# An encoder block on eight cores: LN1 and the squares leave GpSimd, the roots come to it, with a deeper ring and another last tile

## The reference, cut to what matters

```python
proj = einsum('bsd,de->bse', x, w_in)          # 1792 columns: q, k, v, gu, gv
attn = banded_window_attention(q, k, v, sink)  # |t-s| <= 128, 8 query heads on 2 kv heads
gu, gv = gelu(gu), gelu(gv)
sgu = gu * (w_s @ layer_norm(gv) + b)          # in chunks of 128 positions, 8 channel groups
mixed = concat(rms_norm(attn), rms_norm(sgu))  # 512 + 512
x = layer_norm(ALPHA * x + mixed @ w_out)      # LN1
h = square(relu(x @ w_ff1))                    # 4096 wide
x = layer_norm(ALPHA * x + h @ w_ff2)          # LN2
```

## Time and profile before

| what | us |
|---|---|
| median of three runs | 2795.45 (2789.4 to 2796.35) |
| the profiled execution, its own time | 2794.41 |
| its span, core 2, the slowest | 2792.8 |
| the other cores' spans | 2781.2 to 2792.4 |
| TensorE busy in the span | 2645.5 (95%) |
| VectorE, ScalarE, GpSimd busy | 1491.9, 1072.5, 955.4 |

### The profile page before, as it was taken

One profiled execution on the slowest core, in us unless ns is written; L12 is line 12 of the kernel. 1 busy time (PEld: TensorE's weight loads), 2 busy tenths in 40 slices (PEclk: granted clock), 3 DMA queues, 4 the chain that ended last, 5 costly groups with the idle time before them and its releaser, 6 DMA issues.

```text
span 2792.8 us, 57164 instructions; the slowest of 8 cores (2781.2 to 2792.8 us)
## 1 busy us (share of the span) xinstructions
PE 2645.5 (95%) x20844; PEld 1706.4 (61%) x20844; DVE 1491.9 (53%) x2558; ACT 1072.5 (38%) x2241; POOL 955.4 (34%) x661
## 2 busy tenths in 40 slices
PE   4689999999999999999999998899999999999996
PEld 2357777777677777777777676775444444444442
DVE  5876776767777777677767574111222221233222
ACT  4445555555555555555555452221111110111111
...
GB/s 264 220 128 111 103 80 100 110 88 96 99 102 86 107 95 92 100 103 88 107 97 102 80 92 133 156 189 121 151 164 138 147 141 153 177 159 136 157 106 76
DMA packets 110134, 345.81 MB, mean 124 GB/s; under 512 B 11680, under 2 KB 11680, under 8 KB 99744
## 3 DMA queue, kind: packets, MB, share of 16 engines
...
## 4 chain that ended last, share of the span: by engine, by line
PE 78%; ACT 6%; DVE 6%; issue 4%; DMA 4%; POOL 2%; DVEq 0%; ACTq 0%; SPq 0%; POOLq 0%
PE psum L836 27%; PE psum L804 23%; PE psum L760 8%; PE psum L659 4%; PE psum L673 4%; PE psum L675 4%; DMA hsc<-arena 2%; PE psum L729 2%; ACT L678 1%; PE psum L716 1%; DVE arena L689 1%; DMA arena<-w_gu 1%; PE psum L665 1%; PE psum L667 1%; PE psum L754 1%
## 5 line engine op out<-in xcount | busy, mean ns | idle before, releaser
L804 PE MATMUL psum<-arena 128*128 128x256 bf16 x8192 | 999.6, 274 | 15.8 <-ACT arena L648 9.8
L836 PE MATMUL psum<-arena 128*128 128x512 bf16 x4096 | 891.5, 379 | 4.5 <-POOL arena L858 2.3
L804 PEld LDWEIGHTS psum<-arena 128*128 128x128 bf16 x8192 | 773.2, 98 | 163.0 <-issue 56.1
L836 PEld LDWEIGHTS psum<-arena 128*128 128x128 bf16 x4096 | 399.5, 98 | 491.0 <-issue 16.6
L809 POOL TENSOR_TENSOR arena<-arena 128x512 bf16<-128x512 f32 x256 | 268.9, 1050 | 699.8 <-ACT arena L807 402.1
L807 ACT ACTIVATE arena<-psum 128x512 f32<-128x512 f32 x512 | 302.8, 592 | 370.7 <-PE psum L804 341.1
L774 POOL TENSOR_TENSOR arena<-arena 128x1024 f32<-128x1024 f32 x128 | 309.2, 2415 | 301.4 <-DVE arena L771 273.3
L843 DVE SCALAR_TENSOR_TENSOR arena<-psum,arena 128x512 f32<-128x512 f32 x128 | 88.3, 692 | 593.2 <-PE psum L836 521.6
L646 ACT ACTIVATE arena<-arena 128x1 f32<-128x1 f32 x320 | 93.3, 293 | 782.4 <-DVE arena L849 660.1
L856 POOL TENSOR_TENSOR arena<-arena 128x1024 f32<-128x1024 f32 x62 | 145.7, 2351 | 558.9 <-ACT arena L853 558.9
L809 DVE TENSOR_TENSOR arena<-arena 128x512 bf16<-128x512 f32 x256 | 214.7, 838 | 173.4 <-ACT arena L807 90.5
...
## 6 DMA issues: line engine op xcount, KB each, us to landing
hsc<-arena SPq DMA_DIRECT2D x256, 256.0 KB, 2.5
...
arena<-xt POOLq DMA_DIRECT2D x64, 256.0 KB, 5.2
...
```

The costliest lines, as they stand in the source:

```text
L804: R.pe(lambda e, fc=fc, ph=ph, z=z: [e.matmul(ph.ap[:, z * 256:(z + 1) * 256], lhsT=w1q[fc // 4].ap[:, c, (fc % 4) * 128:(fc % 4 + 1) * 12 ...
L836: R.pe(lambda e, s_=s_, q=q: [e.matmul(ps[s_][hf].ap, lhsT=hb[fc // 16].ap[:, fc % 16, s_ * 128:(s_ + 1) * 128], rhs=w2c[fc // 4].ap[:, fc ...
```

## The change

The roots: `rsqrt` now issues two GpSimd operations on one element per partition, an add of the epsilon and a power of -0.5. The `rms_norm` roots take the sum of squares as it is; the factor sqrt(512) goes into the VectorE operation that applies the root. LN1's end is two VectorE operations on 1024 elements, `(y - mean) * G1` and `y * rstd + B1`. The square of bank `k` = 1 is ScalarE's, and each half of a stage has a record of its own. The last three tiles of `ff1` write to a ring of 8 stages that lies over `hT[1]`. In the last tile, `ff2_last` finishes one bank after the other, normalises with the same two VectorE operations per half row, and writes four pieces of 256 KB, from SP and ScalarE in turn.

```diff
+    NHXT = 3
...
+    for g in range(2):
+        ap = A2.alloc(BF16, [16, 256])
+        t = Buf(ap, f"hT1_{g}", extra=A.under(*A2.last))
+        hxgate_w = t.extra
+        flat = ap.rearrange("p a b -> p (a b)")
+        for k in range(4):
+            hx.append(Buf(flat[:, k * 1024:(k + 1) * 1024], f"hx{g}{k}"))
...
-    def rsqrt(src_ap, src_buf, eps_buf, scale, lnb, outb):
-        R.act(lambda e: e.activation(out=lnb.ap, in_=src_ap, func=AF.Ln, bias=eps_buf.ap, scale=scale),
-              [src_buf, eps_buf], [lnb], 60, "el")
-        R.act(lambda e: e.activation(out=outb.ap, in_=lnb.ap, func=AF.Exp, scale=-0.5), [lnb], [outb], 1, "el")
+    def rsqrt(src_ap, src_buf, eps, outb):
+        R.pool(lambda e: e.tensor_scalar(out=outb.ap, in0=src_ap, scalar1=eps, scalar2=None, op0=ALU.add), [src_buf], [outb], 50)
+        R.pool(lambda e: e.tensor_tensor(out=outb.ap, in0=outb.ap, in1=mhalf.ap, op=ALU.pow), [outb, mhalf], [outb], 50)
...
-        R.dve(lambda e: e.tensor_scalar(out=yb.ap, in0=yb.ap, scalar1=mv1[p].ap[:, 0:1], scalar2=rstd1[p].ap,
-                                        op0=ALU.subtract, op1=ALU.mult), [yb, mv1[p], rstd1[p]], [yb], 1024, 2)
-        for (cst, aop) in ((G1, ALU.mult), (B1, ALU.add)):
-            R.pool(lambda e, cst=cst, aop=aop: e.tensor_tensor(out=yb.ap, in0=yb.ap, in1=cst.ap, op=aop), [yb, cst], [yb], 1024)
+        R.dve(lambda e: e.scalar_tensor_tensor(out=yb.ap, in0=yb.ap, scalar=mv1[p].ap[:, 0:1], in1=G1.ap,
+                                               op0=ALU.subtract, op1=ALU.mult), [yb, mv1[p], G1], [yb], 1024)
+        R.dve(lambda e: e.scalar_tensor_tensor(out=yb.ap, in0=yb.ap, scalar=rstd1[p].ap, in1=B1.ap,
+                                               op0=ALU.mult, op1=ALU.add), [yb, rstd1[p], B1], [yb], 1024)
...
+            if i >= NI - NHXT:
+                j = hn[0] % len(hx)
+                hs, h2, hkey, hg = hx[j], hx2[j], f"hx{j}", [hxg]
...
-                eng = R.dve if k == 0 else R.pool
-                eng(lambda e, hs=hs, r_=r_, k=k: e.tensor_tensor(out=hs.ap[:, k * 512:(k + 1) * 512], in0=r_.ap, in1=r_.ap,
-                                                                 op=ALU.mult), [r_], [hs], 512)
+                if k == 0:
+                    R.dve(lambda e, hk=h2[k], r_=r_: e.tensor_tensor(out=hk.ap, in0=r_.ap, in1=r_.ap, op=ALU.mult),
+                          [r_] + hg, [h2[k]], 512)
+                else:
+                    R.act(lambda e, hk=h2[k], r_=r_: e.activation(out=hk.ap, in_=r_.ap, func=AF.Square), [r_] + hg, [h2[k]], 480)
...
+    def ff2_last(i):
...
+        for s_ in range(2):
...
+            for hf in range(2):
...
+                for q in range(8):
+                    R.pe(lambda e, s_=s_, q=q, hf=hf: [e.matmul(ps[s_][hf].ap, lhsT=hb[fc // 16].ap[:, fc % 16, s_ * 128:(s_ + 1) * 128],
...
+                R.dve(lambda e, hf=hf, y_=yh[hf]: e.scalar_tensor_tensor(
+                    out=y_.ap, in0=ps[s_][hf].ap, scalar=1.0 / ALPHA, in1=y_.ap, op0=ALU.mult, op1=ALU.add),
...
+            rsqrt(mvB[p].ap[:, 1:2], mvB[p], EPS / (ALPHA * ALPHA), rstdB[p])
+            for hf in range(2):
+                R.dve(lambda e, hf=hf, p=p, y_=yh[hf]: e.scalar_tensor_tensor(
+                    out=y_.ap, in0=y_.ap, scalar=mvB[p].ap[:, 0:1], in1=G2.ap[:, hf * 512:(hf + 1) * 512],
...
+                R.dma("sp" if hf == 0 else "act", lambda e, s_=s_, hf=hf, y_=yh[hf]: e.dma_start(
```

64 lines of the change are left out of this document (51 added, 13 removed).

## The result

The changed kernel takes 2836.7 us (the median of three runs, 2834.6 to 2837.1; a fourth of 3199.6 us, with cores 4 to 7 at a granted clock of 0.82 to 0.83 in place of 0.98, is left out, as such runs are of every ratio below) where the kernel before takes 2795.7: a ratio of 1.015, 95% interval 1.013 to 1.017. That is 42 us slower, where 30 us faster was predicted, and 47 us above the upper end of the range. In what follows a ratio is turned into us by (ratio - 1) x 2795.

A forecast was written before the change was run, and what follows sets the result against it. TensorE was taken as the bound, busy 1462.4 of 1500 us in the long stretch, with gains only where it waits. Terms -15 - 3 + 0 + 2 + 1 - 14 = -29 took 2794.4 us to 2765, range 2746 to 2790.

The forecast's parts named there:

- The step that failed first: Long stretch, 200 to 1700 us: TensorE does the same matmuls after the change, so at most its idle 37.6 us can be won.
- the root's price: Roots on GpSimd: two operations taken at 0.3 us each, the latency as unchanged from ScalarE's 0.293 + 0.200 us.
- The second rival: Roots come late on GpSimd, queued behind waiting transfers, and hold VectorE: 0.8 us a block, 2816 us; chance 0.13.
- Long stretch, -15: 200 to 1700 us: TensorE's three waits of 24.7 us lose two causes, 15 us off; bounds 25 off or nothing.
- Start, -3: Up to 200 us: casts lose at most 9.2 us of stretching, LN1s add 6.5; -3, between -9 and +5.
- Transition, 0: 1700 to 1780 us: no gain, since the ring serves only later tiles 29 to 31; bounds -8 to +10.
- the bound of +10: Transition's upper bound: ScalarE, now also waiting for the transfers that empty `hst`, holds relus back.
- Handover, +2: Handover to second half: loading `hT[1]` must wait for the last stores of h; +2 us, 0 to 8.
- the last sign of being wrong: The prediction is wrong if TensorE stands still around 1900 us for `hT`.
- Second half, +1: Roots can queue behind GpSimd's wide operations, but TensorE has another tile to work on; +1 us, 0 to 4.
- Tail, -14: Kernel's end: 4.1 us off for gap and slow start, 10.1 in place of 20.1 after; 14 off, 9 to 15.
- the views named as a test: New profile: L689's successor near 0.54 us, casts 0.68 to 0.8, no late gap, 10 us end, `hst` waits remaining.

The follow-up runs named there:

- e1: The changed kernel with the constant -0.5 put in the word of the unused epsA, so later buffers lie 4 bytes lower, as before the change: ratio 1.0064.
- e9: On e1, the planner told GpSimd's measured root times (254 and 740 ns in place of twice 305), only the order changing: ratio 1.0005.
- e7: On e1 with its old planner costs, all roots back on ScalarE as logarithm and exponential: ratio 0.9928.
- e15: On e7, the ring of store slots switched off (NHXT 0), nothing else: ratio 0.9908, 2767.1 us.

## Why the prediction was wrong

**The step that failed first** stands in the first paragraph, on what bounds the kernel: TensorE "does the same matmuls after the change". It does the same ones, but those of seven lines at 2.2 to 2.5 ns more in the mean. The diff had the cause in plain sight, one word allocated ahead of every buffer, and I gave it no cost since no row of before shows an operand's place. It cost 24 to 28 us, in the long stretch 91.0 - 75.4 = 15.6 and in the second half 25.2 - 20.2 = 5.0.

**The second step that failed is the root's price.** I took 0.3 us an operation, between a memset of 0.10 and a wide operation of 2.4; the two took 0.254 and 0.741 in the mean. The prediction itself gave one sign of it: wrong if VectorE shows long waits for roots. The latency was not "unchanged": in the last tile but one of after 1.2 us pass from the end of the statistics to the operation that takes the root. With the planner's price it made the 34 to 38 us of the roots.

The second rival, to which I gave 0.13, said 2816 us, and the change without its word (e1) is at 2813 by its ratio. That nearness is partly luck, since its mechanism, roots held up behind transfers in GpSimd's stream, shows in one root of four. In the long stretch of after (core 4, by the starts in the trace) the roots behind L705, L716 and L787 begin 0.16 to 0.17 us (median) after what they wait for; the attention's, behind L759, begins 0.74 us after it, in 23 blocks with the issue of x's load (L570) in between. Beyond 0.3 us each, these delays make 24 us; in e9 they make 23, so they are not what the planner's price won there.

The terms, by the stages of the table, first with the roots back and the word out (e7), then as changed:

- *Long stretch, -15.* -9.6 in e7, +21.6 as changed. The mechanism was right: the waits for L689's successor and for the relu went, VectorE's operations run at 0.547 us. Two thirds of the size came in e7. With the roots on GpSimd not even that did: the scores' waits, 18.2 us in after, are 18.7 in e1 and 1.7 in e7.
- *Start, -3.* -4.9 in e7, 0.1 in e1, +3.5 as changed. The casts lost 22 x (1.100 - 0.727) = 8.2 us, against 9.2 at most.
- *Transition, 0.* -4.4 in e7, +1.6 as changed, inside its bounds. ScalarE did come to wait for the slots (14.9 us) and to hold relus back, as the bound of +10 had it: TensorE waits 10.4 to 13.5 us for them between 1690 and 1960 us in e7, where it waited 4.2 to 6.9 before (cores 1, 3, 4 and 5). What went in exchange are TensorE's waits in x1's transposes and in `mix` (L785 and L760), 5.3 to 11.7 us before and 0.5 to 2.7 in e7 on the same cores. So two moves against each other stand behind the small sum.
- *Handover, +2.* +8.9 in e7 and +11.8 as changed, past its bound of 8. The term was mis-sized: the ring, whose place under `hT[1]` is what it priced, costs 3 to 8 us in four pairs, and TensorE did stand still for that load, 4.4 us in after (core 4), as the last sign of being wrong had it. Without the ring (e15) the handover still loses 2.5 us more than before, with waits for the relu for which this term had nothing.
- *Second half, +1.* +0.3 in e7, +11.8 as changed: 5 us of the word and 7 of the roots behind GpSimd's wide work, past the bound of 4. The reason given, that TensorE has another tile to work on, failed eight times by about a microsecond.
- *Tail, -14.* -2.8 - 11.4 = -14.2 in e7: right to the microsecond, but by two misses that cancel. The gap and the slow start gave 2.8 of the 4.1 (a gap of 1.13 us is left in e7), and behind the last matmul's end stand 8.8 us against the 10.1 worked out. As changed -9.8: the gap in front of the last 64 matmuls stayed, since GpSimd's wide work came later.

Most of the views named as a test came out as predicted (L707's median, the casts, the end, VectorE's waits for `hst`), the closed gap in front of the last 64 matmuls did not, and none of them sees the rate of a matmul. The last pieces of 256 KB on two queues landed in 2.1 and 2.2 us (medians of two each, after), less than the 2.5 taken. So the 1.7 us that the tail's sum would have been worse by the rule of the Trainium skill, "Trainium Kernel Development and Optimization", Key Constraints, did not come.
